# Attention pairs of a fused two-layer denoising step taken two at a time every second chunk, their probabilities turned inside the products

## What is computed

```python
def window_attn(q, k, v, kc, vc, sink):            # mixer C, 4 query heads, 2 key heads
    s_loc = einsum('bnqhgd,bnjhd->bnhgqj', qb, kw) * scale      # 128 queries, up to 3*128 keys
    s_ctx = einsum('bnqhgd,blhd->bnhgql', qb, kc) * scale       # and 128 context keys
    pr = sink_softmax(concatenate([s_loc, s_ctx], -1), sink)
    o = einsum('bnhgqj,bnjhd->bnqhgd', p_loc, vw) + einsum('bnhgql,blhd->bnqhgd', p_ctx, vc)

def neighbourhood_attn(q, k, v, kc, vc, rpb):      # mixer D, 4 heads, window 8 x 16 + bias
    pr = softmax(concatenate([s_loc + bias, s_ctx], -1))
    ...
def latent_layer(...):
    yc = window_attn(...) * silu(cz)
    yd = neighbourhood_attn(...) * silu(dz)
    y = concatenate([ya, yb, yc, yd], -1) @ w_out
    return x + gate * y
```

## Time and profile before

| | |
|---|---|
| runs | 1227.78, 1230.07, 1232.89 us (median 1230.07) |
| profiled execution, its own time | 1228.56 us |
| its span, first to last instruction | 1226.8 us |
| granted TensorE clock, mean | 0.987 of full speed |
| TensorE busy | 1180.8 us (96%) |
| VectorE busy | 618.2 us (50%) |
| ScalarE busy | 437.2 us (36%) |
| GpSimd busy | 359.1 us (29%) |
| chain of waits that ended last | TensorE 91%, VectorE 4%, ScalarE 1% |

### The profile page before, as it was taken

The page is one execution under the profiler, slowest core; times in us unless marked ns, Lnnn a source line. Parts: engine busy times, 40 slices in busy tenths (PEclk is TensorE's granted clock), DMA queues, the critical chain, the costliest instruction groups (busy, mean ns, idle before and its releaser), DMA issues.

```text
span 1226.8 us, 20333 instructions
## 1 busy us (share of the span) xinstructions
PE 1180.8 (96%) x8022; PEld 1099.6 (90%) x8022; DVE 618.2 (50%) x1412; ACT 437.2 (36%) x1003; POOL 359.1 (29%) x284
## 2 busy tenths in 40 slices
PE   2799999999999999999999999999999999999996
PEld 0589989988988999999999999998888999999996
DVE  3667856655664542152485363765324452224256
ACT  3342445445344111152354344544435411114221
POOL 0123331044250222232452232105424212222342
PEclk9799999999999999999999999999999999999998
DMA  8503211233320112225461110312111011222334
GB/s 332 213 30 132 100 68 57 102 102 103 105 74 18 35 35 104 73 87 169 136 198 53 58 61 21 106 62 72 61 48 57 19 38 49 87 90 77 113 113 157
DMA packets 42862, 110.81 MB, mean 90 GB/s; under 512 B 6032, under 2 KB 21520, under 8 KB 41488
## 3 DMA queue, kind: packets, MB, share of 16 engines
q1 hardware_dynamic: 38736, 105.58, 25.3%
q10 hardware_dynamic: 4032, 3.93, 0.9%
HBM read 99.27 MB, written 10.22 MB: 89 GB/s over the span
## 4 chain that ended last, share of the span: by engine, by line
PE 91%; DVE 4%; ACT 1%; issue 0%; DVEq 0%; ACTq 0%
PE psum L981 72%; PE psum L995 6%; PE psum L1017 5%; PE psum L1005 5%; PE psum L1025 1%; DVE h_lo L1249 1%; DVE slots L1240 1%; PE psum L1034 1%; PE psum L1135 0%; DVE slots L1366 0%; PE psum L1043 0%; ACT h_hi L764 0%; DVE slots L1573 0%; DVE slots L1363 0%; DVE slots L1370 0%; PE psum L189 0%
## 5 line engine op out<-in xcount | busy, mean ns | idle before, releaser
L981 PE MATMUL psum<-h_hi,w_hi 128*128 128x384 f32 x1728 | 596.3, 345 | 6.6 <-DVE h_lo L1249 6.5
L981 PE MATMUL psum<-h_hi,w_lo 128*128 128x384 f32 x1728 | 579.7, 335 | 0.0
L981 PE MATMUL psum<-h_lo,w_hi 128*128 128x384 f32 x1728 | 579.1, 335 | 0.0
L303 POOL TENSOR_TENSOR w_lo<-w_raw,w_hi 128x512 fp32r<-128x512 f32 x144 | 204.0, 1438 | 631.3 <-ACT w_hi L297 631.3
L981 PEld LDWEIGHTS psum<-h_hi,w_hi 128*128 128x128 f32 x1728 | 324.8, 188 | 33.4 <-issue 26.4
L981 PEld LDWEIGHTS psum<-h_lo,w_hi 128*128 128x128 f32 x1728 | 325.5, 188 | 0.0
L981 PEld LDWEIGHTS psum<-h_hi,w_lo 128*128 128x128 f32 x1728 | 325.1, 188 | 0.0
L297 ACT CAST w_hi<-w_raw 128x512 fp32r<-128x512 f32 x144 | 81.9, 618 | 173.3 <-PE psum L981 146.6
L866 ACT ACTIVATE prob<-prob,stat 128x512 f32<-128x512 f32 (+2 forms) x144 | 96.8, 673 | 114.0 <-DVE stat L1436 113.7
L1436 DVE CUSTOM_DVE_ANT_0 prob<-psum,table 128x512 f32<-128x512 f32 (+1 forms) x72 | 43.7, 644 | 81.1 <-PE psum L995 81.1
L1446 DVE TENSOR_SCALAR prob<-prob,stat 128x512 f32<-128x512 f32 (+1 forms) x144 | 81.4, 565 | 5.7
(11 more groups left out here) (108 smaller groups left out, 967.2 us busy)
## 6 DMA issues: line engine op xcount, KB each, us to landing
w_raw<-in_w_tiles SPq DMA_DIRECT2D x72, 512.0 KB, 3.4
xy<-in_w_mod SPq DMA_DIRECT2D x32, 512.0 KB, 4.5
table<-in_rpb SPq DMA_DIRECT2D x48, 192.0 KB, 3.0
slots<-in_w_mod SPq DMA_DIRECT2D x8, 1024.0 KB, 7.7
table<-in_w_tiles SPq DMA_DIRECT2D x16, 512.0 KB, 3.9
xy<-in_xT SPq DMA_DIRECT2D x8, 576.0 KB, 7.6
slots<-in_xT SPq DMA_DIRECT2D x8, 384.0 KB, 4.9
x_kept<-xy SPq DMA_DIRECT2D x8, 384.0 KB, 5.4
```

What stands on the lines that cost most here:

```text
L303: nc.gpsimd.tensor_tensor(w_lo[:, w % 2, a:b], RAW[raw_at(w)][:, a:b], w_hi[:, w % 2, a:b], ALU.subtract).then_inc(s.lo_ready, 1)
L981: last = nc.tensor.matmul(psum[:, bank, 0:CH], a[:, w % 2, k, :], h[:, k, cols], start=(k == order[0] and a is w_hi and h is h_hi), stop=( ...
```

## The change

The pairs of attention are taken two at a time at every second step (a *visit*). S_AT now gives a list of pairs: two pairs at each of the steps 12, 14, ... 28, 30 to 36 and 42 to 48, one pair at 38 and 50: 19 visits in a layer, 17 of them with two pairs. T and V of a visit both belong to step S + 2. T no longer stands after a chunk: the (up to four) units of the visit are turned inside chunk S + 2, one each ahead of the slices 0 to 3. A unit's scores get a bank of their own out of four (banks 3 to 6, `unit_bank`), the turned blocks go back into the bank of their scores, and ScalarE copies them over the probabilities in `prob`; `probT` is gone. V of the two pairs then follows the chunk, in columns 0 to 127 and 128 to 255 of bank 7, and then S of the next visit. V comes ahead of S on TensorE, the gates ahead of the bias on VectorE, and the normalisation stands right behind the bias, ahead of rope, `multiply` and `normalise`. Since V may use columns that `misc` uses, V waits for the read-out of the last `misc` up to its step. A unit's bias waits for V of the unit four earlier, where it waited for its T.

```diff
-        probT = sb("probT", [P, 2, S_W])
-        BANK_S, BANK_T, BANK_O = 3, 5, 7
+        BANK_S, BANK_O = 3, 7
-        S_AT = {12 + p: p for p in range(18)} | {31 + p: 18 + p for p in range(9)} | {43 + p: 27 + p for p in range(9)}
-        T_AT = {s + 2: p for s, p in S_AT.items()}
-        V_AT = {s + 3: p for s, p in S_AT.items()}
-        S_STEP = {p: s for s, p in S_AT.items()}
+        S_AT = ({12 + 2 * j: (2 * j, 2 * j + 1) for j in range(9)}
+                | {30 + 2 * j: (18 + 2 * j, 19 + 2 * j) for j in range(4)} | {38: (26,)}
+                | {42 + 2 * j: (27 + 2 * j, 28 + 2 * j) for j in range(4)} | {50: (35,)})
+        V_AT = {s + 2: pairs for s, pairs in S_AT.items()}
+        S_STEP = {p: s for s, pairs in S_AT.items() for p in pairs}
+        def units_of(pairs):
+            return [2 * p + r for p in pairs for r in range(2)]
+        def unit_bank(u):
+            return BANK_S + u % PROBS
+        def values_at(p):
+            return slice(p % 2 * P, p % 2 * P + P)
...
                 act.wait_ge(s.turned, u + 1)
-                if u >= 2:
-                    act.wait_ge(s.values_ready, u // 2)
-                nc.scalar.copy(probT[:, u % 2, 0:n * P], psum[:, BANK_T + u % 2, 0:n * P]).then_inc(s.copied, 1)
+                nc.scalar.copy(prob[:, u % PROBS, 0:n * P], psum[:, unit_bank(u), 0:n * P]).then_inc(s.copied, 1)
...
-                if g in S_AT:
-                    exp_unit(2 * S_AT[g])
-                    exp_unit(2 * S_AT[g] + 1)
-                if g in T_AT:
-                    copy_probs(2 * T_AT[g])
-                    copy_probs(2 * T_AT[g] + 1)
+                for u in units_of(S_AT.get(g, ())):
+                    exp_unit(u)
+                for u in units_of(V_AT.get(g + 1, ())):
+                    copy_probs(u)
...
             def scores(p):
-                if p >= 1:
-                    pe.wait_ge(s.biased, u)
...
             def turn_probs(u):
                 pe.wait_ge(s.normed, u + 1)
-                if u >= 2:
-                    pe.wait_ge(s.copied, u - 1)
...
             def values(p):
-                pe.wait_ge(s.copied, u + 2)
-                if p >= 1:
-                    pe.wait_ge(s.gated, p)
...
+                turned_here = units_of(V_AT.get(g, ()))
                 for at, k in enumerate(order):
+                    if at < len(turned_here):
+                        turn_probs(turned_here[at])
                     if at == 4:
                         misc(g)
...
-                if g in T_AT:
-                    turn_probs(2 * T_AT[g])
-                    turn_probs(2 * T_AT[g] + 1)
+                if g in V_AT:
+                    first, last = V_AT[g][0], V_AT[g][-1]
...
+                    if misc_at[0] <= g:
+                        misc_free(max(m for m in misc_at if m <= g))
...
+                    pe.wait_ge(s.copied, 2 * last + 2)
+                    if first > 0:
+                        pe.wait_ge(s.gated, first)
+                    for p in V_AT[g]:
+                        values(p)
                 if g in S_AT:
...
-                    scores(p)
-                if g in V_AT:
...
-                    misc_free(g)
...
-                    values(p)
+                    for p in S_AT[g]:
+                        scores(p)
...
                 if u >= PROBS:
-                    dve.wait_ge(s.turned, u - PROBS + 1)
+                    dve.wait_ge(s.values_ready, (u - PROBS) // 2 + 1)
...
                 take_part(n, c)
+                if g in V_AT:
+                    dve.wait_ge(s.values_ready, V_AT[g][-1] + 1)
+                    for p in V_AT[g]:
+                        gate_pair(p)
                 if g in S_AT:
...
-                    bias_unit(2 * p)
-                    bias_unit(2 * p + 1)
-                if g in V_AT:
-                    gate_pair(V_AT[g])
+                    for u in units_of(S_AT[g]):
+                        bias_unit(u)
+                for u in units_of(S_AT.get(g, ())):
+                    norm_unit(u)
                 if g in ROPE_AT:
                     rope(ROPE_AT[g])
...
-                if g in S_AT:
-                    norm_unit(2 * S_AT[g])
-                    norm_unit(2 * S_AT[g] + 1)
                 mods_at(g + 1)
```

More of the change, by code:

```diff
@@ L994, in scores @@
                         src, at, width = parts[r][b]
-                        last = nc.tensor.matmul(psum[:, BANK_S + r, at:at + width], queries(u + r),
+                        last = nc.tensor.matmul(psum[:, unit_bank(u + r), at:at + width], queries(u + r),
                                                 src, start=True, stop=True, skip_group_check=True)
@@ L1001, in turn_probs @@
                 pe.wait_ge(s.normed, u + 1)
-                if u >= 2:
-                    pe.wait_ge(s.copied, u - 1)
                 for b in range(BLOCKS[u]):
-                    last = nc.tensor.transpose(psum[:, BANK_T + u % 2, b * P:(b + 1) * P],
+                    last = nc.tensor.transpose(psum[:, unit_bank(u), b * P:(b + 1) * P],
                                                prob[:, u % PROBS, b * P:(b + 1) * P], ident[:, :])
@@ L1011, in values @@
                 u = 2 * p
-                pe.wait_ge(s.copied, u + 2)
-                if p >= 1:
-                    pe.wait_ge(s.gated, p)
                 for b in range(BLOCKS[u]):
                     for r in range(2):
-                        last = nc.tensor.matmul(psum[64 * r:64 * r + 64, BANK_O, 0:P], unit_values(u + r)[b],
-                                                probT[:, r, b * P:(b + 1) * P], start=(b == 0),
+                        last = nc.tensor.matmul(psum[64 * r:64 * r + 64, BANK_O, values_at(p)], unit_values(u + r)[b],
+                                                prob[:, (u + r) % PROBS, b * P:(b + 1) * P], start=(b == 0),
                                                 stop=(b == BLOCKS[u] - 1), skip_group_check=True)
@@ L1083, in misc @@
                     misc_free(misc_at[at - 1])
-                before = sum(v < g for v in V_AT)
+                before = sum(len(pairs) for v, pairs in V_AT.items() if v < g)
                 if before:
@@ L1161, in tensor_layer @@
                 last.then_inc(s.chunk_done, 1)
-                if g in T_AT:
-                    turn_probs(2 * T_AT[g])
-                    turn_probs(2 * T_AT[g] + 1)
+                if g in V_AT:
+                    first, last = V_AT[g][0], V_AT[g][-1]
+                    if first == 0:
+                        pe.wait_ge(s.cv_natural, 3)
+                    if misc_at[0] <= g:
+                        misc_free(max(m for m in misc_at if m <= g))
+                    if first == 2 * GROUP_P:
+                        pe.wait_ge(s.cache0_in, 16 * (layer + 1))
+                        pe.wait_ge(s.dv_natural, 6)
+                    if first == 3 * GROUP_P:
+                        pe.wait_ge(s.cache1_in, 16 * (layer + 1))
+                        pe.wait_ge(s.dv_natural, 12)
+                    pe.wait_ge(s.copied, 2 * last + 2)
[3 more added lines that the diff above has]
+                        values(p)
                 if g in S_AT:
-                    p = S_AT[g]
-                    if p == 0:
+                    first, last = S_AT[g][0], S_AT[g][-1]
+                    if first == 0:
                         pe.wait_ge(s.layer_in, 16 * LAYER_IN * (layer + 1))
                         pe.wait_ge(s.rope_ready, 2)
-                    if p == GROUP_P:
+                    if first <= GROUP_P <= last:
                         pe.wait_ge(s.rope_ready, 3)
-                    if p == 2 * GROUP_P:
+                    if first == 2 * GROUP_P:
                         part_read(s, pe, NO["dk", 0])
@@ L1176, in tensor_layer @@
                             part_read(s, pe, NO["dq", 0], b)
-                    if p == 3 * GROUP_P:
+                    if first == 3 * GROUP_P:
                         part_read(s, pe, NO["dk", 1])
@@ L1180, in tensor_layer @@
                             part_read(s, pe, NO["dq", 1], b)
-                    scores(p)
-                if g in V_AT:
-                    p = V_AT[g]
-                    if p == 0:
-                        pe.wait_ge(s.cv_natural, 3)
-                    misc_free(g)
[L1187 to L1192, removed]
-                    values(p)
+                    for p in S_AT[g]:
+                        scores(p)
             order = Y_ORDER
@@ L1435, in bias_unit @@
                     bias = table[:, bias_table(u) % TABLES if i < LT else 0, 0:width]
-                nc.vector.tensor_tensor_reduce(out=row[:, 0:width], in0=psum[:, BANK_S + r, 0:width], in1=bias,
+                nc.vector.tensor_tensor_reduce(out=row[:, 0:width], in0=psum[:, unit_bank(u), 0:width], in1=bias,
                                                scale=1.0, scalar=first, op0=ALU.add, op1=ALU.min,
@@ L1449, in gate_pair @@
                 mixer, i, t, _ = UNITS[2 * pair]
-                dve.wait_ge(s.values_ready, pair + 1)
```

(9 more changed lines are left out.)

## The result

The changed kernel takes 1212.37 us (median of 4 runs, 1210.44 to 1213.69) against 1230.47 for the kernel before: a ratio of 0.9852, 95% interval 0.9827 to 0.9878, or 18.1 us between the medians. The profiled execution took 1213.18 us, its span is 1211.2, 15.6 us under the span before. In the listing after, the products are L986, scores L998, transposes of probabilities L1006, values L1015, small transposes L1023 and L1049, the tile sum L1041.

What follows compares the result with a forecast made beforehand. TensorE, busy without waits in attention, was taken as the bound; passage losses falling from 41.0 to 22.8 us take 18.2 off the profiled 1228.56, giving 1210.4, and 1.5 between scales makes 1211 us, range 1206 to 1222.

Steps and rivals of the forecast that it cites:

- The bound: Attention: TensorE waits for nothing, so time falls only if it does less or loses less between its matmuls.
- the sum: Attention of both layers: losses at passages 41.0 us before and 22.8 us after, a gain of 18.2 us.
- The price list: TensorE's loss per passage: T 0.08, S 0.19, V 0.15, products' head 0.11, products into S or V 0.09 us.
- V straight into S: Passage between blocks, 34 times: priced at V's 0.15 us; bounds 5 us more gain or 4 us less.
- Cover: Attention visits: moved work finds cover, VectorE slack 1.5 us or more, ScalarE cover 1.3 us.
- the first rival: Short stalls in tight visits: T or V 0.3 us late 38 times, 11 us back, 1222; chance 0.10.
- a sign of being wrong: Changed profile: idle TensorE ahead of a transpose with VectorE's normalisation as releaser, among other signs.
- stop the stream: Rival 2, transposes inside a chunk: 144 interruptions at 0.34 us, 49 us, 1258; chance 0.05.
- late normalisation at every visit: Rival 3, VectorE beside GpSimd: unit 3 0.6 us late 38 times, 23 us, 1234, no gain; chance 0.05.
- its shown duration: Rival 4, transposes broken up inside chunks: each costs its 0.27 us duration, 82 us on top, 1293; chance 0.01.
- The drain: TensorE: by the skill a change of tiling mode drains the engine, so V into S drains like the others.

Runs made afterwards that it cites:

- the kernel with the multiplies moved: Changed kernel with layer 0's first modulation multiplies at later steps and their sums and turns one step later: 1209.54 us, again 1210.86 us.
- one-pair kernel: Changed kernel with one pair at every step instead of two at every second, units still turned inside the chunk: 1228.26 us.
- V, S, V, S: Changed kernel with V and S of the two pairs alternating in a visit instead of V, V, S, S: 1224.48 us.

## Why the prediction was right

- *The bound.* TensorE was busy without gaps, so only its own losses could go, and they did: the attention stretches fell by 17.3 us, and the sum had 18.2. That it came so near is in part luck. Without the waits of layer 0, which the sum put at nothing, the stretches fall by 20.1 us (598.5 less 578.4, the kernel with the multiplies moved): the passages gave 1.9 more than the sum, and the waits took 2.8. The 18.1 us between the medians owe something to the spread of the runs as well: the two spans differ by 15.6, and the medians, when the changed kernel was run again, by 16.2.
- *The price list.* Four of the five entries that the table above compares came out as forecast, the fifth (S) 0.01 below. Over all the blocks no entry is off by more than some 0.01 us (T's way out lost 0.09 where the list has 0.08, S 0.20 where it has 0.19); over as many places as the sum counts, that is most of the 1.9 us. The one passage that the trace before did not show, V straight into S, cost its nearest row: V's block loses 0.15 with S behind it as with products behind it. Neither end of its bounds came near.
- *Where the gain stands.* The sum gave 16.4 of its 18.2 us to 44 fewer returns to products and to 34 fewer S and V blocks each; what T no longer loses on its way out goes for the most part into 28 more exits from products into V or S and the 0.01 for each of 144 groups inside chunks. The one-pair kernel shows that, and V, S, V, S shows that every change of form costs, not only leaving the products.
- *Cover.* This is the step that fell short: the slack of 1.5 us on VectorE did not hold in two visits of layer 0, where `multiply` of step 11 (until 114.7) and the rope of step 15 (until 142.1) still run when the bias could start; and I did not look at who waits for the last `multiply`, which comes later now that the normalisation stands ahead of it. That is the tile sum of step 20, 1.4 us. Together 2.1 us idle and 2.8 from start to start, where the sum had nothing. It is the first rival at three places instead of 38, and idle TensorE ahead of a transpose, which the forecast named as a sign of being wrong, did show at two of them.
- *The other rivals.* Transposes among products do not stop the stream: 0.01 us a group, and 0.11 for one more. A late normalisation at every visit did not happen. What late normalisations cost is shown, the whole gain in 14 waits, but there rope and `multiply` made them late, not GpSimd. Slow ones beside GpSimd did come: ahead of the last `multiply`, with GpSimd at the bias tables, three of the four took 0.80 to 1.06 us instead of 0.42 to 0.49, together 1.5 us longer, about what the tile sum then waited. That the sum would not have waited without them was not tested. A transpose in a chunk costs 0.11, not the 0.27 of its shown duration. The Trainium skill, TensorE: Matmul & The Clock Gate, Part 4: PE-mode transpose, has about 275 ns in one kernel's context; that agrees here with the length of a row and not with its price.
- *The drain.* The Trainium skill, TensorEngine Tiling (Array Packing), Key Properties, says that a change of tiling mode drains the engine and that a change of tile within a mode does not. The runs agree as to the time that it costs, and give the price: 0.09 to 0.10 us on the way out, and 0.05 to 0.11 at the head of what follows. Within a block of V, whose matmuls change the tile at every step, a pair of them takes the bare 0.11 us. That it is a drain that takes this time, no row shows.

## What to carry to other kernels

On an engine that is busy all the time, price the passages: read from start to start what stands between blocks of different form, multiply by the number of passages before and after, and most of the change's worth is there before it is built; the waits are not in it. Group work by the array's form, put jobs of a form among work of the same form, and count the passages that remain: moving one job may only move its loss. Then check who waits for each instruction that comes later now, also in the few steps that are unlike the running ones.

## What the runs showed of the hardware that was not expected

The head of a block depends on what comes first: behind a 64-row block, a transpose of 128 columns as the first matmul of the full form lost 0.05 to 0.06 us (0.41 for four where 0.36 stands among products), a product of 384 columns 0.11. And a wait on TensorE costs more than its idle time: 2.8 us from start to start where 2.1 are shown as idle, and 18.7 where 14.6 are shown.
